# A fused three-branch decoder layer on one core: carried states in place of off-diagonal scores in gated linear attention

## The reference

```python
def gla_chunk_step(S, xs):              # gated linear attention, 4 heads, DK = 128, DV = 256
    q, k, v, g = xs
    G = jnp.cumsum(g, axis=2)
    ...                                 # decay[t,s,:] = exp(G_t - G_s) for s <= t, else 0
    A = jnp.einsum("bhtk,bhtsk,bhsk->bhts", q, decay, k)
    o = jnp.einsum("bhtk,bhkv->bhtv", q * jnp.exp(G), S) + jnp.einsum("bhts,bhsv->bhtv", A, v)
    S_new = jnp.exp(G_last[:, :, 0, :])[..., None] * S + jnp.einsum(
        "bhsk,bhsv->bhkv", k * jnp.exp(G_last - G), v)
    return S_new, o

def hybrid_layer(h, p, t5_table):
    xn = rms_norm(h, p["g_pre_mix"])
    z = xn @ p["w_in"] + p["b_in"]
    ...                                 # the columns of z: GLA, sparse attention, mLSTM, three gates
    mix = sigmoid(gate_a) * y_a + sigmoid(gate_b) * y_b + sigmoid(gate_c) * y_c
    h = h + rms_norm(mix @ p["w_out"], p["g_post_mix"])
    xn = rms_norm(h, p["g_pre_mlp"])
    u = jnp.square(jax.nn.relu(xn @ p["w_up"]))
    return h + rms_norm(u @ p["w_down"], p["g_post_mlp"])
```

## Time and profile before

| | us |
|---|---|
| median of 3 runs | 1294.49 (1294.04 to 1294.63) |
| the profiled execution | 1293.61 |
| its span | 1291.9 |
| PE busy | 1280.8 (99%) |
| PEld busy | 1042.3 (81%) |
| POOL busy | 768.2 (59%) |
| DVE busy | 602.7 (47%) |
| ACT busy | 398.0 (31%) |

### The profile page before, as it was taken

How to read it: one execution, slowest core, us unless ns; L and a number is a source line. 1 busy time by engine, 2 the same in 40 slices (tenths; PEclk the granted TensorE clock), 3 DMA queues, 4 the chain that set the end, 5 groups by cost and what they waited for, 6 DMA issues and landing times.

```text
span 1291.9 us, 17528 instructions
## 1 busy us (share of the span) xinstructions
PE 1280.8 (99%) x6604; PEld 1042.3 (81%) x6604; DVE 602.7 (47%) x1086; ACT 398.0 (31%) x822; POOL 768.2 (59%) x919
## 2 busy tenths in 40 slices
PE   9999999999999999999999999999999999999998
PEld 8866887677898889777898987787888888888886
DVE  4248788642275766734545563241611111333434
ACT  5243555533013323434032334311511111212322
POOL 8737430125654543656864446786576676788882
PEclk9999999999999999999999999999999999999999
DMA  7745200223321222222343333443233333222221
GB/s 193 229 153 172 81 2 26 67 65 91 98 76 56 66 58 58 66 82 66 99 105 91 82 99 98 143 135 96 63 103 92 89 97 114 87 93 98 98 82 66
DMA packets 168445, 120.59 MB, mean 93 GB/s; under 512 B 12394, under 2 KB 146640, under 8 KB 168361
## 3 DMA queue, kind: packets, MB, share of 16 engines
q1 hardware_dynamic: 161654, 108.32, 28.9%
q10 hardware_dynamic: 6706, 11.15, 2.7%
HBM read 115.20 MB, written 9.62 MB: 97 GB/s over the span
## 4 chain that ended last, share of the span: by engine, by line
PE 98%; DVE 1%; ACT 1%; issue 0%; ACTq 0%
PE GP L1827 45%; PE GP L1862 9%; PE PA L1862 9%; PE GP L1842 7%; PE GP L1824 7%; PE PA L2026 3%; PE GP L2088 3%; PE PA L2230 2%; PE PA L2125 2%; PE PA L2063 1%; PE PA L2137 1%; PE GP L1907 1%; PE PA L1996 1%; PE PA L2222 1%; PE GP L2301 1%; PE PA L2027 1%
## 5 line engine op out<-in xcount | busy, mean ns | idle before, releaser
L622 POOL TENSOR_TENSOR wlo<-wraw,whi 128x256 fp32r<-128x256 f32 x712 | 566.1, 826 | 14.8
L618 POOL TENSOR_SCALAR whi<-wraw 128x1024 fp32r<-128x1024 f32 x178 | 194.9, 1095 | 484.0 <-PE GP L1827 248.6
L1827 PE MATMUL GP<-xh,whi 128*128 128x512 f32 x352 | 147.1, 418 | 0.0
L1827 PE MATMUL GP<-xh,wlo 128*128 128x512 f32 x352 | 139.1, 395 | 0.0
L1827 PE MATMUL GP<-xl,whi 128*128 128x512 f32 x352 | 138.8, 394 | 0.0
L1770 DVE TENSOR_TENSOR ul<-U,uh 128x512 fp32r<-128x512 f32 x64 | 65.0, 1051 | 109.7 <-ACT uh L1152 109.7
L1827 PE MATMUL GP<-nh,whi 128*128 128x512 f32 x240 | 95.1, 396 | 0.0
L1827 PE MATMUL GP<-nl,whi 128*128 128x512 f32 x240 | 95.1, 396 | 0.0
L1827 PE MATMUL GP<-nh,wlo 128*128 128x512 f32 x240 | 95.1, 396 | 0.0
L1774 DVE SCALAR_TENSOR_TENSOR U<-GP,rrow 128x512 f32<-128x512 f32 x32 | 22.1, 692 | 141.7 <-PE GP L1827 140.3
L1827 PEld LDWEIGHTS GP<-xh,whi 128*128 128x128 f32 x352 | 66.2, 188 | 17.3 <-issue 2.9
(11 more groups left out here) (406 smaller groups left out, 2789.9 us busy)
## 6 DMA issues: line engine op xcount, KB each, us to landing
wraw<-in_w_in SPq DMA_DIRECT2D x75, 512.0 KB, 3.8
wraw<-in_w_up SPq DMA_DIRECT2D x32, 512.0 KB, 4.0
wraw<-in_w_down SPq DMA_DIRECT2D x32, 512.0 KB, 3.5
line_rows<-bias_line SPq DMA_DIRECT2D x8, 655.0 KB, 5.2
table<-line_rows SPq DMA_DIRECT2D x4, 1024.0 KB, 5.2
wraw<-in_w_br_dsa SPq DMA_DIRECT2D x8, 512.0 KB, 4.0
wraw<-in_w_br_gla SPq DMA_DIRECT2D x8, 512.0 KB, 3.9
wraw<-in_w_br_ml SPq DMA_DIRECT2D x8, 512.0 KB, 4.1
```

The source lines that it names most:

```text
L618: nc.gpsimd.tensor_scalar(hi, src, 1.0, 1.0, ALU.mult, ALU.mult).then_inc(hi_done, 1)
L622: part = nc.gpsimd.tensor_tensor(lo[:, at:to], src[:, at:to], hi[:, at:to].bitcast(FP32), ALU.subtract)
L1827: ins = mm(ps[0:t.m, 0:SEQ], wt[:, s0, w], av, start=st, stop=sp_)
```

## The change

**In GLA** what a query takes from tokens ahead of its own tile no longer goes through scores. The decayed keys of the meta tokens and of tiles 0 to 2 (`km`, `KHt`) are transposed by TensorE, copied out by ScalarE in one piece (`keysT`), and multiplied with the values, 256 columns each, into PSUM. VectorE sums the results with a decay into four carried states (`states`, 128x256 each, one for each query tile). `weighted` then adds, for each tile and half, scores of the tile by values and the state by `QQ`, 128 columns each. `states` and `keysT` lie in the part of `AT` that held the scores. `QQ` isn't rescaled any more.

**Level operands.** Keys in the last block of B of a tile are in no pair of level l, so the stationary operand has 128 - B columns: 64, 96, 112, 120, 124, 126 and 127 in place of 128.

**Index scores.** The wait for each `iq` stands in the loop, ahead of the first score that reads it.

**The boundary to the MLP.** The last token tile is handled in two halves: VectorE makes its first half of `xn`, then the low parts of tile 2, then its second half; TensorE transposes the first half, runs a half up tile, and transposes the second.

**The end.** VectorE multiplies by the gain while ScalarE still works on the root, and needs one operation fewer behind it.

```diff
@@ -390,6 +390,7 @@
 later = ATm
+states, keysT = AT[:, :, P:P + DV], AT[:, :, P + DV:SEQ]
@@ -853,8 +854,7 @@
 if h:
-    act.wait_ge(od_q, 4 * h)
-    act.wait_ge(od_ps, 4 * h)
+    act.wait_ge(av_ps, h)
@@ -864,14 +864,8 @@
 def off_out(h):
-    if h:
-        act.wait_ge(av_ps, h)
-    for q, j in enumerate([2, 1, 0]):
-        act.wait_ge(od_ps, 4 * h + q + 1)
-        w = SEQ - P * (j + 1)
-        nc.scalar.activation(AT[:, j, P:P + w], bank(q)[:, 0:w], ACT.Copy).then_inc(od_ev, 1)
-    act.wait_ge(od_ps, 4 * h + 4)
-    nc.scalar.activation(ATm[:, :], bank(3), ACT.Copy).then_inc(od_ev, 1)
+    act.wait_ge(od_ps, 3 * h + 1)
+    nc.scalar.activation(keysT, bank(0).rearrange("p (t n) -> p t n", t=QT), ACT.Copy).then_inc(od_ev, 1)
@@ -1141,8 +1135,8 @@
 projected(3)
+high_norm(2)
 residual(2)
-high_norm(2)
@@ -1163,8 +1157,10 @@
 act.wait_ge(tok_done, QT + t + 1)
-act.wait_ge(d0_ss, t + 1)
-root(2, t, accumulators("down", 1, t)).then_inc(o_ss, 1)
+nc.scalar.activation(jk[:, :], accumulators("down", 1, t), ACT.Square, accum_out=ssf[:, 2, t, 1:2]).then_inc(d0_ss, 1)
+act.wait_ge(d0_ss, QT + t + 1)
+seq(nc.scalar.activation(ssf[:, 2, t, 0:1], ssf[:, 2, t, 1:2], ACT.Ln, bias=ssf[:, 2, t, 0:1], scale=1.0 / D))
+nc.scalar.activation(ssf[:, 2, t, 0:1], ssf[:, 2, t, 0:1], ACT.Exp, scale=-0.5).then_inc(o_ss, 1)
@@ -1448,9 +1444,10 @@
 B = LEVELS[l]
-o_ = AT[:, :, 0:P].rearrange("p t (n two b) -> p t n two b", two=2, b=B)[:, :, :, 1, :]
-m_ = lm[:, l, :].rearrange("p (n b) -> p n b", b=B).unsqueeze(1).broadcast_to([P, QT, 64 // B, B])
-d_ = bank(k % 4)[:, 0:QT * 64].rearrange("p (t n b) -> p t n b", t=QT, b=B)
+n_ = P - B
+o_ = AT[0:n_, :, 0:P].rearrange("p t (n two b) -> p t n two b", two=2, b=B)[:, :, :, 1, :]
+m_ = lm[0:n_, l, :].rearrange("p (n b) -> p n b", b=B).unsqueeze(1).broadcast_to([n_, QT, 64 // B, B])
+d_ = bank(k % 4)[0:n_, 0:QT * 64].rearrange("p (t n b) -> p t n b", t=QT, b=B)
@@ -1459,19 +1456,23 @@
 dve.wait_ge(od_e, 6 * h + 6)
-seq(tt(KHt[:, :], KHt[:, :], kh[:, h % 2, 0:ALL - P], ALU.mult))
+tt(KHt[:, :], KHt[:, :], kh[:, h % 2, 0:ALL - P], ALU.mult).then_inc(od_q, 1)
+dve.wait_ge(od_q, 6 * h + 1)
 twice(km[:, h % 2, 0:2 * META], KHt[:, 0:META], km_ok)
 tt(QQ[:, :], QQ[:, :], qh[:, h % 2, :], ALU.mult).then_inc(od_q, 1)
-for q, j in enumerate([2, 1, 0]):
-    dve.wait_ge(od_ps, 4 * h + q + 1)
-    dve.wait_ge(od_q, 4 * h + q + 1)
-    ts(QQ[:, (j + 1) * P:SEQ], QQ[:, (j + 1) * P:SEQ], gf[:, j + 1:j + 2], None, ALU.mult).then_inc(od_q, 1)
-    if q == 0 and h + 1 < HEADS:
-        values("gv", h + 1, 0)
-    if q == 1 and h + 1 < HEADS:
-        forget_sums(h + 1)
+if h + 1 < HEADS:
+    values("gv", h + 1, 0)
+    forget_sums(h + 1)
 if h:
     low_parts(0, h - 1)
+dve.wait_ge(od_ps, 3 * h + 2)
+nc.vector.tensor_copy(states[:, 0, :], bank(1)[:, 0:DV]).then_inc(od_q, 1)
+for j in range(QT - 1):
+    if j == 1:
+        dve.wait_ge(od_ps, 3 * h + 3)
+    dve.wait_ge(od_q, 6 * h + 3 + j)
+    u_ = bank(1 + (j + 1) // 2)[:, (j + 1) % 2 * DV:((j + 1) % 2 + 1) * DV]
+    stt(states[:, j + 1, :], states[:, j, :], gf[:, j + 1:j + 2], u_, ALU.mult, ALU.add).then_inc(od_q, 1)
@@ -1730,10 +1731,10 @@
-def residual_scaled(t):
+def residual_scaled(t, which=range(2)):
     dve.wait_ge(o_ss, t + 1)
     dve.wait_ge(g0_ok, t + 1)
-    for hf in range(2):
+    for hf in which:
@@ -1757,8 +1758,9 @@
 low_norm(1)
-residual_scaled(3)
+residual_scaled(3, [0])
 low_norm(2)
+residual_scaled(3, [1])
@@ -1784,11 +1786,12 @@
 for t in range(QT):
+    dve.wait_ge(d0_ss, QT + t + 1)
+    r_ = ssf[:, 2, t, 0:1]
+    seq(tt(xn[:, t, 0:SEQ], accumulators("down", 1, t), gains[:, 0, SEQ:D], ALU.mult))
     dve.wait_ge(o_ss, QT + t + 1)
-    ps, r_ = accumulators("down", 1, t), ssf[:, 2, t, 0:1]
     stt(hres[:, t, 0:SEQ], accumulators("down", 0, t), r_, hres[:, t, 0:SEQ], ALU.mult, ALU.add).then_inc(fin, 1)
-    seq(stt(ps, ps, r_, gains[:, 0, SEQ:D], ALU.mult, ALU.mult))
-    tt(hres[:, t, SEQ:D], ps, hres[:, t, SEQ:D], ALU.add).then_inc(fin, 1)
+    stt(hres[:, t, SEQ:D], xn[:, t, 0:SEQ], r_, hres[:, t, SEQ:D], ALU.mult, ALU.add).then_inc(fin, 1)
@@ -1985,11 +1988,11 @@
 pe.wait_ge(rk_ok, 2)
-for m in range(4):
-    evacuated(f"iq{m}")
 for v in range(SCORES):
     i, h = 1 + v // IDX_H, v % IDX_H
     n_, w = TILE_ROWS[i], TILE_KEYS[i]
+    if v < IDX_H and v % 2 == 0:
+        evacuated(f"iq{v // 2}")
@@ -2122,7 +2125,8 @@
 b = (7 * h + l) % 2
-ins = mm(bank(k % 4)[:, i * 64:(i + 1) * 64], KL[:, b, i * P:(i + 1) * P], QL[:, b, i * 64:(i + 1) * 64],
+n_ = P - LEVELS[l]
+ins = mm(bank(k % 4)[0:n_, i * 64:(i + 1) * 64], KL[:, b, i * P:i * P + n_], QL[:, b, i * 64:(i + 1) * 64],
@@ -2132,11 +2136,10 @@
 for v in range(2):
-    c = slice(v * P, (v + 1) * P)
     for j in range(QT):
-        mm(bank(v)[:, j * P:SEQ], vh[:, h % 2, j, c], AT[:, j, 0:SEQ - j * P], start=(j == 0), stop=False)
-    pe.wait_ge(od_ev, 4 * h + 4)
-    ins = mm(bank(v), vm[:, h % 2, c], ATm[:, :], start=False, stop=True)
+        o_ = bank(v)[:, j * P:(j + 1) * P]
+        mm(o_, vh[:, h % 2, j, v * P:(v + 1) * P], AT[:, j, 0:P], start=True, stop=False)
+        ins = mm(o_, states[:, j, v * P:(v + 1) * P], QQ[:, j * P:(j + 1) * P], start=False, stop=True)
@@ -2175,18 +2178,24 @@
 pe.wait_ge(lv_sel, 8 * h + 8)
-for q, j in enumerate([2, 1, 0]):
-    pe.wait_ge(od_q, 4 * h + q + 1)
-    mm(bank(q)[:, 0:SEQ - (j + 1) * P], KHt[:, META + j * P:META + (j + 1) * P], QQ[:, (j + 1) * P:SEQ],
-       start=True, stop=True).then_inc(od_ps, 1)
-    if q < 2:
-        nxt("gvB", q)
+pe.wait_ge(od_q, 6 * h + 1)
+pe.wait_ge(km_ok, h + 1)
+nc.tensor.transpose(bank(0)[:, 0:P], km[:, h % 2, :], ident[:, :])
+for j in range(QT - 1):
+    ins = nc.tensor.transpose(bank(0)[:, (j + 1) * P:(j + 2) * P], KHt[:, META + j * P:META + (j + 1) * P], ident[:, :])
+ins.then_inc(od_ps, 1)
+nxt("gvB", 0)
+pe.wait_ge(od_ev, h + 1)
+evacuated(f"gv{h}A", f"gv{h}B", f"gv{h}M")
+mm(bank(1)[:, 0:DV], keysT[:, 0, :], vm[:, h % 2, :], start=True, stop=True)
+for j in range(QT - 1):
+    o_ = bank(1 + (j + 1) // 2)[:, (j + 1) % 2 * DV:((j + 1) % 2 + 1) * DV]
+    ins = mm(o_, keysT[:, j + 1, :], vh[:, h % 2, j, :], start=True, stop=True)
+    if j % 2 == 0:
+        ins.then_inc(od_ps, 1)
+nxt("gvB", 1)
 nxt("gvM")
-pe.wait_ge(od_q, 4 * h + 4)
-pe.wait_ge(km_ok, h + 1)
-mm(bank(3), km[:, h % 2, :], QQ[:, :], start=True, stop=True).then_inc(od_ps, 1)
-pe.wait_ge(od_ev, 4 * h + 3)
-evacuated(f"gv{h}A", f"gv{h}B", f"gv{h}M")
+pe.wait_ge(od_q, 6 * h + 6)
@@ -2277,9 +2286,9 @@
-def transposed(t):
-    for hf in range(2):
+def transposed(t, which=range(2)):
+    for hf in which:
@@ -2297,6 +2306,8 @@
 for k in range(KT):
+    if hf and k == KT // 2:
+        pe.wait_ge(nl_ok, 8)
@@ -2314,10 +2325,11 @@
 half("up0", 0)
-transposed(3)
+transposed(3, [0])
 pe.wait_ge(nl_ok, 6)
 half("up1", 0)
-pe.wait_ge(nl_ok, 8)
+transposed(3, [1])
+pe.wait_ge(nl_ok, 7)
```

## The result

The changed kernel takes **1279.28 us** (median of 4 runs, 1278.92 to 1279.91) against 1294.49 before: a ratio of 0.9884 [0.9868, 0.9899], 15.2 us less. In a second series, with a chip of its own, it took 1278.74 (4 runs) against 1294.24, a ratio of 0.9883 [0.9869, 0.9896], 15.5 us less. The forecast was 1277.7, in a range of 1275.5 to 1281.5. The profiled execution took 1279.91 us (span 1278.2).

The account below looks back on a forecast made before the run. TensorE, 99% busy, was taken as the bound. Gains of 10.0 + 3.3 + 0.85 + 2.1 + 0.55 = 16.8 us off 1293.61 gave 1276.8, and 0.9 for the median 1277.7 us, range 1275.5 to 1281.5.

Parts of the forecast that it names:

- What bounds the kernel: Whole kernel: TensorE, busy 99% of the span, so time goes only where it issues less or stands still less.
- States: GLA, ahead of the tile: carried states in place of scores save 2.51 us a head, 10.0 us in four.
- 128-column matmuls bound by loads: GLA, `weighted`: loads set the pace of sixteen matmuls a head, 6.6 us lost, 1284.3 us; chance 0.03.
- States late: GLA, a head's end: VectorE makes the states too late for TensorE, 7.5 us lost, 1285.2 us; chance 0.05.
- Narrower operands: GLA levels: shorter loads save 0.206 us times four tiles and four heads, 3.3 us; lower bound 0.
- A drain at level 0: GLA level 0: changing tiling mode leaves a 0.19 us load open twice a head, 1.5 us, 1279.2 us; chance 0.03.
- Loads no longer beside a matmul: GLA levels: each of 224 narrow loads shows at its whole 0.191 us, 31.6 us more, 1312.6 us; chance 0.03.
- Index scores: Ahead of the first index score: the wait asks for the first projection alone, saving 0.85 us; lower bound 0.
- boundary: Boundary to the MLP: half an up tile fills TensorE's idle 2.4 us, saving 2.1 us, between 0.8 and 2.4.
- end: End of the kernel: gain product moves ahead and two VectorE operations follow, saving 0.55 us, from 0.4 to 0.7.

Follow-up runs that it names:

- g_late: The changed kernel with VectorE's copy and sums for the states moved behind two more pieces of the next head's values; 1292.19 us (10 runs).
- micro: A separate kernel computing nothing of the layer, only streams of float32 matmuls between float32r ones; 0.218 us a matmul at 128 stationary, 64 moving columns.
- b_narrow: The kernel before with the narrower level operands alone; 1293.82 us (11 runs), ratio 0.9993.
- a_states: The kernel before with the carried states alone, level operands, index scores, boundary and end as before; 1285.23 us (4 runs), ratio 0.993.

## Why the prediction was right, and where its sizes were off

- **What bounds the kernel** was right: TensorE's 99%, and all gains where it issues less or waits less.
- **States: right.** 9.70 us of 10.0. Inside, with what each leaves to the row behind it, transposes took 0.44 us (0.50 forecast), products 1.72 (1.73), `weighted` 3.57 (3.48): 5.73 in place of 5.71. A head gained 2.42 us and not 2.51; the 0.07 that these terms leave over were not attributed.
- **128-column matmuls bound by loads** (rival): refuted. Sixteen at 0.223 us in the kernel, at 0.218 by themselves. The Trainium skill's 81 ns from issue to issue (TensorE: Matmul & The Clock Gate, section Back-to-back issue gap) would be 0.32 us for four passes, an estimate; the trace does not agree. The prediction counted four loads in the 0.87 us that it set against this; the trace has eight, two for each of the four matmuls (32 in the four heads, 0.192 us each), so nothing of the refutation rests on that count.
- **States late** (rival): did not occur, with 3.3 us to spare where 1.6 or more was forecast. The copy takes 0.42 us and each sum 0.53, not the bound of 0.8. But the rival was priced without the clock: g_late shows that 7.5 us of waiting, the figure it was given, costs 13.2.
- **Narrower operands: the term that was mis-sized**, 3.3 us where 2.07 came. Level 0 was to give 0.40 us a head and gave 0.09: its four matmuls take 0.61 us and not 0.44, 0.09 goes at the entry and 0.05 in the piece behind. The prediction took the moving columns' 0.108 us as the floor, and inside a stream that nearly holds (0.116 in micro). What its sum left out is what a group of 64-column operands costs at its ends, 0.15 us in the group and 0.10 ahead of it in micro, and only four matmuls share it. Levels 1 to 6 give 0.19, 0.10, 0.05, 0.02, 0.01 and 0.01, 0.37 a head where 0.43 was forecast. So the slope of the loads in the earlier trace rows was read rightly, 0.85 ns a column twice in a matmul (micro: 0.218 to 0.167 us for 32 columns is 0.80).
- **A drain at level 0** (rival): right in the main, though it was given 0.03 and against it stood an observation that holds still. A 32-column operand of float32r comes and goes at 0.12 us, as in the earlier trace rows and above at 412.71. A float32 group of 64 columns costs 0.25 us at its ends in micro, and 0.05 more in the float32 piece behind it in the kernel, where the rival was priced at 0.38 a head. Four heads make 1.0 to 1.2 us, most of the 1.2 that this term fell short by, and the rival's 1279.2 us is nearer to what was measured than the forecast's 1277.7: that the time lies in the range does not make this part of the mechanism right. The Trainium skill (TensorEngine Tiling (Array Packing), section Key Properties) says that a change of tiling mode drains TensorE; the runs agree for float32, where 96 columns pay nothing and 64 and 32 do, and disagree for float32r. That the cost is such a drain, and not something else of operands this narrow, was not shown. Evidence on one data type was carried over to another.
- **Loads no longer beside a matmul** (the slower rival): refuted. Level 1 at 96 columns is 0.19 us a head shorter, not longer.
- **Index scores, boundary, end:** 0.84, 2.03 and 0.56 us for 0.85, 2.1 and 0.55. The second half of the boundary's transposes (L2294) starts at 917.55, behind half an up tile, with no wait listed.

What the prediction missed is that taking this wait away also keeps the clock: without the split, most of the narrower operands' gain is lost behind it in nine runs of eleven (b_narrow).

## What to carry to other kernels

Price a change on a bound TensorE in columns where columns move slowly enough, and in loads below about 128 moving columns; the two rates from the timeline, start to start, gave 10.0 us for 9.7. A pace is not the price of a group: where few matmuls of another shape stand among others, look for what their ends cost, and do not carry an observation from one data type to another. Both are in the one term that was wrong. A wait on the critical engine can cost more than its length, since the clock may fall behind it, so take out the longest waits first, and test small gains with those gone.

## What the runs showed of the hardware

- float32 matmuls with a fresh stationary operand, 16 in a row, 64 moving columns: 0.218 us at 128 stationary columns, 0.167 at 96, 0.125 at 64, 0.119 at 32, ends included.
- A group of float32 matmuls with 64 stationary columns costs 0.10 us on entry and 0.15 more at its ends, beside 0.116 for each matmul; 32 columns cost the same 0.10 on entry. At 96 and 128 there is no such cost, and for float32r operands of 32 columns none was seen.
- Behind a wait of 2.5 us TensorE went on at 1.2 GHz (granted clock 0.50), three times of three, and lost 1.7 us; behind 0.9 us it did not, three times of three; behind the boundary's waits it did in the profile of b_narrow and, by the mean clock, in nine of its eleven runs, and did not in the profiles of the kernel before and of a_states.
- TensorE's first 26 records took from 4.52 to 5.92 us in eleven profiled executions, as their pace rose from one in 0.213 us to one in 0.112 earlier or later, which is 1.4 us of difference between profiles that no edit made.
